# Third mixer: convolution one channel block after another in PSUM, output product in two halves; openings with three groups

## What is computed

```python
def even_mixer_2(t, layer_idx, w_in, ..., w_out, cos, sin):
    proj = t @ w_in                                     # 1024 -> 3*512 + 2*512
    y_a = diff_attention(proj[..., :1536], ...)         # 4 heads, two maps each
    y_b = conformer_conv(proj[..., 1536:], ...)
    return jnp.concatenate([y_a, y_b], axis=-1) @ w_out # 1024 -> 1024

def conformer_conv(g, dw_w, dw_b, ln_g, ln_b):
    u = g[..., :512] * jax.nn.sigmoid(g[..., 512:])
    y = conv(u, dw_w[:, None, :], padding=(30, 0), groups=512) + dw_b    # 31 taps, one filter per channel
    return jax.nn.silu(layernorm(y, ln_g, ln_b))

# diff_attention: rotary on q and k; per block of 128 queries, both maps of a head:
#   p = softmax(mask(q @ k.T / 8)); w = p[0] - lam * p[1]; o = w @ v
# then rmsnorm(o, subln) * 0.8 per head
```

## Time and profile before

| | |
|---|---|
| median of three executions | 2150.46 us (2149.64 to 2152.09) |
| profiled execution | 2150.88 us |
| its span, first to last instruction | 2149.1 us |
| PE busy | 1833.9 us (85% of the span) |
| DVE / ACT / POOL busy | 939.5 / 759.3 / 932.5 us |
| mean granted PE clock | 0.918 of 2.4 GHz |
| third mixer, first product to first update of the next stage | 713.58 to 1036.11 us |

### The profile page before, as it was taken

One profiled execution on the slowest core, in us unless ns is written; L12 is line 12 of the kernel. 1 busy time (PEld: TensorE's weight loads), 2 busy tenths in 40 slices (PEclk: granted clock), 3 DMA queues, 4 the chain that ended last, 5 costly groups with the idle time before them and its releaser, 6 DMA issues.

```text
span 2149.1 us, 19907 instructions
## 1 busy us (share of the span) xinstructions
PE 1833.9 (85%) x7392; PEld 1351.6 (63%) x7392; DVE 939.5 (44%) x1443; ACT 759.3 (35%) x1245; POOL 932.5 (43%) x1100
## 2 busy tenths in 40 slices
PE   5999988997567886757899999986778879999996
PEld 4766556776445664525688888864333557888885
DVE  1042235546653469563431323358566253214234
ACT  3254454344334422345422222342232343322222
POOL 3433123674442452203465656637331225656563
PEclk9999999998788998868999999998777889999999
DMA  4212002222000221101233233321000112333231
GB/s 161 89 59 62 27 30 87 69 91 67 20 11 30 69 79 39 39 1 49 69 94 97 94 98 98 98 80 38 10 10 10 40 49 88 98 95 96 93 99 69
DMA packets 39552, 139.88 MB, mean 65 GB/s; under 512 B 4512, under 2 KB 4640, under 8 KB 39328
## 3 DMA queue, kind: packets, MB, share of 16 engines
q1 hardware_dynamic: 39456, 138.61, 20.3%
HBM read 136.50 MB, written 2.10 MB: 64 GB/s over the span
## 4 chain that ended last, share of the span: by engine, by line
PE 71%; DVE 17%; ACT 8%; issue 3%; POOL 1%; DMA 0%; SPq 0%; DVEq 0%; ACTq 0%; POOLq 0%
PE ps L540 18%; PE ps L541 17%; PE ps L542 17%; DVE arena L1630 3%; PE ps L569 2%; PE ps L553 1%; PE ps L554 1%; PE ps L555 1%; PE ps L2018 1%; PE ps L788 1%; PE ps L790 1%; POOL ml_scratch L1450 1%; PE ps L2042 1%; PE ps L781 1%; PE ps L2000 1%
## 5 line engine op out<-in xcount | busy, mean ns | idle before, releaser
L2497 POOL TENSOR_TENSOR wl<-raw,wh 128x256 fp32r<-128x256 f32 x988 | 809.6, 851 | 1060.3 <-ACT wh L594 1060.1
L540 PE MATMUL ps<-hh,wh 128*128 128x512 f32 x1204 | 511.2, 425 | 54.2 <-DVE hl L657 46.0
L594 ACT ACTIVATE wh<-raw 128x1024 fp32r<-128x1024 f32 x247 | 261.0, 1057 | 623.7 <-PE ps L542 593.2
L542 PE MATMUL ps<-hh,wl 128*128 128x512 f32 x1204 | 476.2, 396 | 0.0
L541 PE MATMUL ps<-hl,wh 128*128 128x512 f32 x1204 | 476.2, 395 | 0.0
L540 PEld LDWEIGHTS ps<-hh,wh 128*128 128x128 f32 x1204 | 231.4, 192 | 134.7 <-DVE hl L657 55.6
L540 PE MATMUL ps<-mh,wh 128*128 128x512 f32 x632 | 262.3, 415 | 38.3 <-DVE ml L1681 12.3
L541 PEld LDWEIGHTS ps<-hl,wh 128*128 128x128 f32 x1204 | 231.0, 192 | 60.1 <-issue 15.8
L542 PEld LDWEIGHTS ps<-hh,wl 128*128 128x128 f32 x1204 | 230.2, 191 | 49.7
L541 PE MATMUL ps<-ml,wh 128*128 128x512 f32 x632 | 252.5, 399 | 0.0
L542 PE MATMUL ps<-mh,wl 128*128 128x512 f32 x632 | 251.8, 398 | 0.0
(11 more groups left out here) (466 smaller groups left out, 2310.6 us busy)
## 6 DMA issues: line engine op xcount, KB each, us to landing
raw<-in_w SPq DMA_DIRECT2D x247, 512.0 KB, 3.5
x<-in_x SPq DMA_DIRECT2D x8, 256.0 KB, 6.6
out<-x SPq DMA_DIRECT2D x8, 256.0 KB, 2.0
arena<-in_rope SPq DMA_DIRECT2D x3, 512.0 KB, 3.2
arena<-in_dec SPq DMA_DIRECT2D x1, 1024.0 KB, 11.2
mats<-in_mats SPq DMA_DIRECT2D x1, 576.0 KB, 7.4
arena<-in_lw SPq DMA_DIRECT2D x1, 512.0 KB, 3.7
arena<-in_levels SPq DMA_DIRECT2D x1, 448.0 KB, 4.4
```

The lines of the kernel that those rows point to most:

```text
L540: e.matmul(ps[b][:], a, xh, start=first, stop=False)
L542: e.matmul(ps[b][:], l, xh, start=False, stop=final).then_inc(pe.sem, pe.up(*step))
L594: e.activation(wh[:, n % NHL, :], raw[:, n % NRAW, :], ACT.Copy).then_inc(rounded.sem, rounded.up(n))
L2497: e.tensor_tensor(wl[:, n % NHL, cut(i, 2)], raw[:, n % NRAW, cut(i, 2)], wh[:, n % NHL, cut(i, 2)].bitcast(F32), SUB).then_inc(split.sem, ...
```

## The change

1. Openings of all stages but `ssm` do the products of three groups per k. Their PSUM banks are 0, 1, 2; the third group no longer follows the opening. In `diff` `ub` has bank 1 alone, `ua` 0 and 2.
2. The convolution's accumulators are PSUM banks 4, 5, 2 and 3; only the last tap writes SBUF. Block j is done in one piece, tap after tap, and starts behind `um 0`: 8 steps beside `ub 1`, 26 beside `dv`, 44 beside the other `u` groups, 16 beside the first two heads' rotations, 30 beside the rest. `dv` comes before `ua 2`. `lb` comes behind the 78th step.
3. The first half of the attention is merged with the last two heads' rotations only; layer norm and `fn` stand among the values of heads 0 and 1 and the second half of the attention.
4. The output product is split: `p` (channels of the convolution, k 4 to 7) merged behind the `fn` steps, its last 12 steps behind the values of heads 2 and 3, then `v3` of all heads, then `closing(4)`. The attention's row blocks use `mh`, `ml` 0 to 3 as scratch instead of 4 to 7.

```diff
-def opening(a, b):
+def opening(*gs):
...
-        out += [("w", a, k), ("w", b, k), ("sq", k)]
+        out += [("w", g, k) for g in gs] + [("sq", k)]
...
 def steps_even():
-    out = opening(sq[0], sq[1]) + [("e", sq[0]), ("e", sq[1])] + groups(sq[2:] + sk, 8, "e")
+    out = opening(*sq[:3]) + merge(group(sq[3], 8), [("e", g) for g in sq[:3]]) + [("e", sq[3])] + groups(sk, 8, "e")
...
 def steps_odd():
-    out = opening(lx[0], lx[1]) + [("e", lx[0]), ("e", lx[1]), ("bd", 0)]
-    out += group(lx[2], 8, ("bd", 1), ("e", lx[2])) + group(lx[3], 8, ("bd", 2), ("e", lx[3]), ("bd", 3))
+    out = opening(*lx[:3]) + [("e", lx[0]), ("e", lx[1]), ("bd", 0), ("bd", 1), ("e", lx[2])]
+    out += group(lx[3], 8, ("bd", 2), ("e", lx[3]), ("bd", 3))
...
 def steps_diff():
-    ab = [(g, j) for j in range(4) for g in ("ua", "ub")]
-    out = opening(ab[0], ab[1]) + [("e", ab[0]), ("e", ab[1]), ("um", 0)]
-    for j in range(1, 4):
-        out += group(ab[2 * j], 8, ("e", ab[2 * j])) + group(ab[2 * j + 1], 8, ("e", ab[2 * j + 1]), ("um", j))
-    out += [("lb",)]
+    u = [group(("ua", j), 8, ("e", ("ua", j))) + group(("ub", j), 8, ("e", ("ub", j)), ("um", j)) for j in range(4)]
+    out = opening(("ua", 0), ("ub", 0), ("ua", 1)) + [("e", ("ua", 0)), ("e", ("ub", 0)), ("um", 0), ("e", ("ua", 1))]
+    u[1] = u[1][9:]
...
-    values = [[(n, h) for n in ("v1", "v2", "v3") for h in (2 * i, 2 * i + 1)] for i in range(2)]
-    conv = [("cv", j, q) for q in range(31) for j in range(4)]
-    out += merge(qk[0] + merge(qk[1] + v, rows[0]) + values[0] + rows[1] + values[1], conv)
-    out += [("ln", n) for n in range(3)]
-    out += [("fn", n, j) for n in range(4) for j in range(4)]
-    return out + closing(8)
+    values = [[(n, h) for n in ("v1", "v2") for h in (2 * i, 2 * i + 1)] for i in range(2)]
+    conv = [("cv", j, q) for j in range(4) for q in range(31)]
+    out += merge(u[1], conv[:8]) + merge(v, conv[8:34]) + merge(u[2] + u[3], conv[34:78]) + [("lb",)]
+    out += merge(qk[0], conv[78:94]) + merge(merge(qk[1], rows[0]), conv[94:])
+    norm = [("ln", n) for n in range(3)] + [("fn", n, j) for n in range(4) for j in range(4)]
+    part = groups([("p", d) for d in range(KT)], 4, "pe")
+    out += merge(values[0] + rows[1], norm + part[:-12]) + values[1] + part[-12:] + [("v3", h) for h in range(4)]
+    return out + closing(4)
...
 def steps_ffn():
             if f == 0:
-                mul = opening(g, u)
+                mul = opening(g, u, ("fg", 1))
+            elif f == 1:
+                mul = merge(group(u, 8), pend)
...
 BANKS
-    "diff": {"ua": (0, 2), "ub": (1, 3), "dq": (0,), "dk": (1,), "o": (0, 1, 2, 3)},
+    "diff": {"ua": (0, 2, 0, 0), "ub": (1,), "dq": (0,), "dk": (1,), "p": (0, 1), "o": (0, 1, 2, 3)},
...
-PARTED = {"even", "odd", "ffn0", "ffn1", "ssm"}
+PARTED = {"even", "odd", "diff", "ffn0", "ffn1", "ssm"}
...
         def rows_at(n):
-            return mh_[:, 4 + n % 4, :], ml_[:, 4 + n % 4, :]
+            return mh_[:, n % 4, :], ml_[:, n % 4, :]
+        conv_in = [ps[b][:] for b in (4, 5, 2, 3)]
...
 pe_diff
-                if kind == "w" and step[1][0] == "o":
+                if kind == "w" and step[1][0] in "op":
+                    k0 = 4 if step[1][0] == "p" else 0
                     if step[1][1] == 0:
-                        e.wait_ge(dve.sem, dve["mixed", step[2]])
-                    pe_out(e, "diff", step, 0, 8)
+                        e.wait_ge(dve.sem, dve["mixed", k0 + step[2]])
+                    pe_out(e, "diff", step, k0, 4)
...
 dve_diff
                     if q == 0:
                         e.wait_ge(pool.sem, pool["um", j])
-                        e.tensor_scalar(yb[:, j, :], du[:, j, 0:T], V("dww", j), V("dwb", j), MUL, ADD).then_inc(
+                        if j == 2:
+                            e.wait_ge(act.sem, act["te", "dv", 3])
+                        e.tensor_scalar(conv_in[j], du[:, j, 0:T], V("dww", j), V("dwb", j), MUL, ADD).then_inc(
                             dve.sem, dve.up(*step))
                     else:
                         e.wait_ge(dve.sem, dve["cv", j, q - 1])
-                        e.scalar_tensor_tensor(out=yb[:, j, :], in0=du[:, j, q:q + T], scalar=V("dww", 4 * q + j), in1=yb[:, j, :],
-                                               op0=MUL, op1=ADD).then_inc(dve.sem, dve.up(*step))
+                        e.scalar_tensor_tensor(out=yb[:, j, :] if q == 30 else conv_in[j], in0=du[:, j, q:q + T],
+                                               scalar=V("dww", 4 * q + j), in1=conv_in[j], op0=MUL, op1=ADD).then_inc(
+                            dve.sem, dve.up(*step))
...
 act_diff
                 elif kind == "v3":
                     h = step[1]
+                    e.wait_ge(pe.sem, pe["r4", 12 + h])
                     e.wait_ge(dve.sem, dve["mix", h])
                     e.activation(mh[:, h, :], dq4[:, h, :], ACT.Copy).then_inc(act.sem, act.up("mix", h))
+                elif kind == "pe":
+                    g = step[1]
+                    e.wait_ge(pe.sem, pe["w", g, 3])
+                    e.activation(hh_[:, g[1], :], ps[bank("diff", g)][:], ACT.Copy).then_inc(act.sem, act.up("e", g))
```

More of the change, by code:

```diff
@@ L310, in weights @@
         first = {"ua": 1536, "ub": 2048, "dq": 0, "dk": 512, "dv": 1024}
-        return ("l0_w_out_2", 0, 128 * j) if kind == "o" else ("l0_w_in_2", 0, first[kind] + 128 * j)
+        if kind in "op":
+            return ("l0_w_out_2", 4 if kind == "p" else 0, 128 * j)
+        return ("l0_w_in_2", 0, first[kind] + 128 * j)
     layer = {"ffn0": "l0", "ffn1": "l1", "ssm": "l1"}[stage]
@@ L514, in addend @@
         def addend(stage):
-            return hh_ if stage in ("even", "odd") else y
+            return hh_ if stage in ("even", "odd", "diff") else y
         busy = {}
@@ L1683, in dve_diff @@
                 else:
-                    dve_norms(e, "diff", step, 8)
+                    dve_norms(e, "diff", step, 4)
         def act_diff(e):
```

22 lines of the change are left out of this document (12 added, 10 removed).

## The result

The changed kernel took 2132.64 us (median of four executions, 2131.91 to 2138.07), beside 2151.28 us for the kernel before in the same set. The ratio is 0.9917, with a 95% interval of 0.9896 to 0.9937: faster by 0.8%. The forecast was 2127.8 us in a range of 2108 to 2146. The profiled execution took 2131.91 us for a span of 2130.1, 19.0 less than the 2149.1 of before.

The account below looks back on a forecast made before the run. The third mixer was taken as bound in turn by PE, DVE's convolution, attention round trips and the wait before 64 products. Third mixer -21.1 and openings -2.0 gave -23.1 from 2150.88: 2127.8 us, range 2108 to 2146.

Parts of the forecast that it names:

- Openings, -2.0: Openings of three groups: the third group fills five small PE gaps where `lo` is late, 2.0 us gained.
- Start of the convolution: Third mixer: transposes at 740.95, then copy, evictions, sigmoid and `um`, so the first convolution step starts at 745.0.
- The step: One dependent convolution multiply-add on PSUM: 0.74 plus 0.03 for dependence, 0.77 us; ends 0.66 and 1.10.
- D: Rival: convolution in PSUM is slow on DVE; at 1.10 per step +41 us, 2169; chance 0.09.
- T0: End of the third mixer's first attention half, summed along DVE's work from 745.0: 894.4.
- PE's wait costs nothing, as DVE is the later one: Third mixer: PE's wait of some 11 us at `lb` adds nothing to the time.
- T0 to the last product: Six terms from the first attention half's end, 113.6, plus 3.0 for the clock: 116.6 us, ending at 1011.0.
- The 3.0 added for the clock: Allowance of 3.0 us for PE's clock at half after idle stretches, between first attention half and last product.
- A: Rival: the convolution's dependent chain costs nothing, steps 0.66 apart, 13.6 us less, 2114; chance 0.12.
- B: Rival: layer norm and gates fit into the row blocks' waits, 26.7 becomes 17.9, time 2119; chance 0.14.
- C: Rival: products slow the second attention half, PE at its lower level, maxima about 10 us later, 2138; chance 0.18.
- The sum: Whole program: -21.1 us for the third mixer and -2.0 for openings, -23.1, giving 2127.8 us.

Follow-up runs that it names:

- run 1: Kernel before, with only the three-group openings of even, odd, ffn0 and ffn1 added: 2154.65 us, ratio 1.0008.
- run 6: Changed kernel with the convolution's accumulators back in SBUF, block after block order kept: 2147.43 us, ratio 0.9976.
- run 7: Changed kernel with the lambda step ahead of the last two pairs of u groups and the Exp/Ln table reloaded before the first exponentials: 2128.75 us, ratio 0.9892.
- run 10: Changed kernel with `v3` early, the lambda step inside the opening, and the convolution's blocks taking turns: 2118.28 us, ratio 0.9844.
- run 8: Changed kernel with the third mixer's output product in one piece behind the attention: 2146.99 us, ratio 0.9974.
- run 3: Changed kernel with `v3` of heads 0 and 1 before the values of heads 2 and 3, the others among the last twelve product steps: 2122.65 us.
- run 9: Changed kernel with `v3` early and the lambda step inside the third mixer's opening, Exp/Ln table reloaded before the first exponentials: 2112.93 us, ratio 0.9825.

## Why the prediction was right, and where it was not

- **Openings, -2.0: the step that failed.** The steps outside the third mixer cost 3.1 us in place of giving 2.0, run 1 rules out a gain, and its openings grew by their own matmuls and no more. Two faults. The gaps were mis-sized: behind the 1.04 the next two starts are 0.34 apart, where they are 0.63 in the other blocks, so that gap is 0.3 (from `sq` to L541 it is 1.38, against 1.09 elsewhere) and not 0.6; by the distances of the `sq` matmuls all of them are 0.6 us, not 2.0. And I took the time in an opening as fixed, where PE's level moves it by up to 1.4 us from one execution to the next.
- **Start of the convolution**, 745.0: it was 746.17, since the transposes came at 742.17 and not at 740.95: 0.8 of it because the mixer itself began later (714.40 against 713.58), 0.4 by a longer opening.
- **The step**, 0.74 + 0.03: 0.756 + 0.035 = 0.79. The estimate of a dependence at 0.03 past the end holds, and run 6 shows that D's bound was not far-fetched: in SBUF it was 0.909.
- **T0**, 894.4: the last step starts at 894.14 and ends at 894.88. The sum came out in part by luck. The convolution began 1.2 late; its steps took 93.4 us instead of 95.5, although a dependent one was dearer than forecast, because only 83 of the 124 follow another step directly; rotations, row blocks, evictions, the lambda step and the waits took 55.2 instead of 53.9. And "PE's wait costs nothing, as DVE is the later one" was wrong by 3.4 us (run 7). DVE is later on the whole, yet its stall of 4.65 came from PE. I had put 3.5 us of such waiting into the sum and given it to PE's groups, without asking what made PE late.
- **T0 to the last product**, 116.6. It ended at 1010.65, where the forecast had 1011.0. Term by term: first maxima at 914.68, T0 + 19.8 (22.0 forecast); the next four row blocks 29.6 (26.7); the last four 19.7 (20.3); values to the last copy 17.3 (17.4); `v3` 7.6 (7.3); the products left 21.7 (19.9). The 3.0 added for the clock is close to the 2.1 by which the terms together were exceeded, but this is luck and not a clock measured: most of the excess is the 2.9 of the first four row blocks, and there the overlap was mis-sized. From one row block's maxima to the next took 5.3, 4.8, 3.5 and 4.3 us before, and 10.2, 5.8, 10.5 and 3.2 now. So the gates cost 4.9 in front of the second block (5.8 forecast) and the splits 7.0 in front of the fourth (8.0), each a little less than forecast; but by the forecast's prices only 2.1 of them fell into the loop's own waits, and not 5.0.
- **Rivals.** A: its price per step was nearly right (0.13 for 0.11), but run 10 shows a mixer shorter by only 1.6 where the freed steps alone are 6.8, so its 2114 was out of reach. B fell with the 29.6 us. C fell with run 8. D fell with 757 ns at most.
- **The sum.** -22.1 for the mixer where the forecast had -21.1; the forecast missed the median by 4.8. In the two profiles the steps outside the mixer are 5.1 us off and the mixer 1.0 the other way. The last 0.7 are the distance of the changed kernel's median from its profiled execution (2132.64 and 2131.91). The forecast itself starts from the profiled 2150.88 of before, although it notes that the median is 0.4 lower. Two terms were also added up 0.2 wrong each (110.5 - 88 x 0.76 is 43.6, 29 x 0.68 is 19.7).

## What to carry to other kernels

A chain of DVE operations beside GpSimd's work belongs in PSUM, with one SBUF input. Taken out singly, PSUM was worth 16.6 us of the mixer and the split of the product 15.0, together 31.6, and the whole change only 22.1; if they add, the remaining parts of the change cost 9.5 us (an estimate from runs 6 and 8). The late `v3` (5.8, run 3) and the late `lb` (3.4, run 7) account for 9.2 of it. After such a change look for the operations that now stand behind the wrong thing in an in-order queue: removing the two long waits for `v3` and `lb` made this mixer 11.9 us shorter (run 9), over half of what the change itself brought. When an Exp, Ln or Sigmoid changes its place on ACT, count the table loads. And read a gain of a few us from the length of the stage that was changed, not from the total, and even there distrust what is under 2.5 us.
